# Modulation weights multiplied beside layer 0's MLP by GpSimd instead of beside its first projection by TensorE

## The chip, the cores and the metric

One core of a Trainium2 chip runs the program. The metric is the time of one execution on the device, in microseconds (us).

## The reference, cut to what matters

A diffusion backbone of two layers works on 1024 latent and 256 context tokens of 1024 features, in float32. Layer 0 is attention (GQA beside MLA) followed by a squared-ReLU MLP, layer 1 is a long convolution beside a state-space scan, again followed by an MLP. Every sub-layer is modulated by vectors that depend on the conditioning alone:

```
cond_x = silu(c);  cond_c = silu(c_ctx)
for i in range(2):
    mx = split(cond_x @ ada_w[i] + ada_b[i], 6)      # shift, scale, gate of mixer, then of MLP
    mc = split(cond_c @ ada_w[i] + ada_b[i], 6)      # the same for the context stream
    hx = rms_norm(x, g[0]) * (1 + mx[1]) + mx[0]
    x = x + mx[2] * rms_norm(mixer(hx), g[1])
    x = x + mx[5] * rms_norm(mlp(rms_norm(x, g[2]) * (1 + mx[4]) + mx[3]), g[3])
    # the context stream the same way in layer 0; in layer 1 only its first shift and scale are needed
```

`ada_w` is 1024 x 6144 for each layer. The kernel handles it in 12 pieces of 1024 x 512 (2 MB) for each layer, 24 in all. Pieces 0 and 1 are the mixer's shift, 2 and 3 its scale, 4 and 5 its gate, 6 to 11 the same three for the MLP.

## The kernel before, in words

Tokens are cut into three chunks of 512, 512 and 256 columns; features lie in eight tiles of 128 partitions. An exact product is made of three fp32r matmuls for each pair of tiles: weight high part by data high part, high by low, low by high. So each weight tile is rounded by ScalarE (ACT) and its rest is made by VectorE (DVE), `w_low = w_raw - w_high`. Engines run their own instruction lists in order and meet in semaphores; all DMAs are issued by SyncE (SP), in the order of its list.

**The modulation** (class `Modulation`, L102 to L181). For one piece: `load` (L132, a 2 MB DMA into a ring of three), `multiply` (L143: eight matmuls on TensorE (PE), conditioning as weights, four column groups side by side; each shows as two records), `copy` (L153: ACT, PSUM to rows), `turn` (L162: four matmuls that turn the rows into columns), `bias` (L173 on DVE, with L179 or L181 where a norm's gain is folded in).

**The opening** (`opening`, L189). The norm of x: squares (ACT L266), their sum over features (PE L241), the root (ACT L273, L275), scaling (DVE L322), shift and high part (ACT L284), low part (DVE L327), chunk after chunk. The first four pieces of `ada_w` come before anything can be scaled. Pieces 4 to 9 of the list `ADA_FIRST` are made between: ACT copies one after each third shift (`AFTER`). ACT's list squares all eight tiles of chunk 1, then shifts four of chunk 0, takes the root, shifts the other four, and so on.

**The first projection** (`project_attention`, L400): 5 weight tiles by 3 chunks are 15 steps, each 24 matmuls (L396), the sum of squares by head (L476) and the swap for the rotary part (L483), two steps behind. In each of the first 14 steps PE also runs `ada.turn(step - 1)` and `ada.multiply(step)` for the 14 pieces of `ADA_LATER`.

**The joined stage** (`out_and_mlp`, L1316), once for each layer, is one list of steps. In layer 0: steps 0 to 23 are the output projection (eight weight tiles for each chunk, L1568), 24 to 87 the MLP of chunk 0, 88 to 151 that of chunk 1, 152 to 215 that of chunk 2, which has 256 columns; 216 to 227 the next layer's projection. In an MLP four steps "up" (L1581) and four "down" (L1598) alternate. Weights (512 KB a step, SP L1470) go through two raw buffers: the load for step i + 3 waits until DVE has split the tile of step i + 1 (L1741), ACT rounds it (L1648). Norm jobs run beside: POOL (GpSimd) adds the squares of the output (L1853) and of x (L1878) and adds the stream to gated output (L1870); DVE gates (L1759), scales (L1783) and makes low parts (L1752). On PE, `spread_sums` (L1546, L1556) sums what POOL has added, inside a step:

```
pe.wait_ge(added_out, (KT - 1) * (q + 1) - closing[q])
...
pe.wait_ge(added_x, (KT - 1) * (q + 1))
```

Job 0, the norm of chunk 0 ahead of its MLP, has its gates and squares at steps 8 to 13, beside the output projection. ACT squares an output tile into one of two buffers and so waits until POOL has added the tile two before it.

## Time and profile before

| | |
|---|---|
| three runs | 3461.07, 3456.45, 3459.39 us; median 3459.39 |
| profiled execution, first to last instruction | 3457.7 us |
| its time around that span | not recorded apart; the median is 1.7 us above the span |
| PE, DVE, ACT, POOL busy | 96%, 53%, 37%, 20% of the span |
| mean granted TensorE clock | 0.984 of full speed |

A busy share is an average over stages; which engine sets the pace of a stage is read from the waits and the timeline of that stage. In the profile a time stands in us from the start of the span, and "idle before" is the time for which the engine did nothing ahead of an instruction, with the name of what it waited for.

### The profile page before, as it was taken

The numbers are of one execution on the slowest core, as the hardware profiler recorded it, in microseconds if no ns is written. First come the engines' busy times: TensorE is split into PE (matmuls) and PEld (weight loads), VectorE is DVE, ScalarE is ACT, GpSimd is POOL, SyncE is SP. The second block draws the span as 40 slices with busy tenths as digits, with TensorE's granted clock in tenths as the row PEclk, the third lists the DMA queues.
The fourth block names the chain that finished last, engine by engine and source line by source line (L and its number), as shares of the span: only waits on it lengthen the run. The fifth ranks groups of instructions, "written<-read, shape, count | busy, mean of one in ns | idle before, by whom it ended". The sixth has DMA issues, their size and how long they took to land. (4 is left out here: it accounts for less than half of the span.)

```text
span 3457.7 us, 39533 instructions
## 1 busy us (share of the span) xinstructions
PE 3317.7 (96%) x15472; PEld 2443.2 (71%) x15472; DVE 1818.6 (53%) x2304; ACT 1291.3 (37%) x2118; POOL 691.5 (20%) x383
## 2 busy tenths in 40 slices
PE   6999999999999999999999999898999999999998
PEld 3666444555788888888889878652456788888886
DVE  3233544433555544554586444588576654445444
ACT  4333344445553333333454223452113532233332
POOL 0000478667331101300120100110011320002001
PEclk8999999999999999999999999999999999999999
DMA  8753533321253333433465311102513333333333
GB/s 329 290 214 103 179 65 77 77 61 48 98 171 127 112 97 97 146 98 96 131 195 175 113 62 39 51 1 101 203 49 109 132 126 97 98 98 117 121 98 104
DMA packets 134552, 406.62 MB, mean 118 GB/s; under 512 B 24153, under 2 KB 38265, under 8 KB 130016
## 3 DMA queue, kind: packets, MB, share of 16 engines
q1 hardware_dynamic: 134368, 404.11, 36.1%
q8 instruction: 123, 2.02, 0.2%
q14 instruction: 61, 0.50, 0.0%
HBM read 345.05 MB, written 58.92 MB: 117 GB/s over the span
## 5 line engine op out<-in xcount | busy, mean ns | idle before, releaser
L1598 PE MATMUL psum<-hid_high,w_high_and_low 128*128 128x512 f32 (+1 forms) x1536 | 416.3, 356 | 11.7 <-DVE hid_low L1831 9.4
L1581 PE MATMUL psum<-h_high,w_high_and_low 128*128 128x512 f32 (+1 forms) x1536 | 415.6, 356 | 0.7 <-DVE w_high_and_low L1741 0.7
L1648 ACT ACTIVATE w_high_and_low<-w_raw 128x1024 fp32r<-128x1024 f32 x226 | 238.6, 1056 | 342.3 <-PE psum L1598 238.8
L1853 POOL TENSOR_TENSOR squares_then_rstd_of_out<-squares_then_rstd_of_out,square_out 128x512 f32<-128x512 f32 (+1 forms) x69 | 103.2, 1495 | 1277.1 <-ACT square_out L1663 1277.1
L1741 DVE TENSOR_TENSOR w_high_and_low<-w_raw,w_high_and_low 128x1024 fp32r<-128x1024 f32 x226 | 285.7, 1265 | 90.9 <-ACT w_high_and_low L1648 90.2
L1313 POOL TENSOR_TENSOR probs_added<-probs_added,probs_turned 128x1024 f32<-128x1024 f32 x128 | 308.1, 2407 | 66.6 <-ACT probs_turned L1238 54.0
L1598 PEld LDWEIGHTS psum<-hid_high,w_high_and_low 128*128 128x128 f32 x1536 | 274.2, 190 | 54.5 <-DVE hid_low L1831 7.8
L1581 PEld LDWEIGHTS psum<-h_high,w_high_and_low 128*128 128x128 f32 x1536 | 273.1, 189 | 42.5 <-DVE w_high_and_low L1741 1.3
L1280 DVE TENSOR_REDUCE row_max<-psum 128x1 f32<-128x1280 f32 x120 | 179.0, 1492 | 228.5 <-PE psum L1176 137.2
L1828 DVE TENSOR_TENSOR hid_high<-hid_relu_and_square 128x512 fp32r<-128x512 f32 (+1 forms) x160 | 111.5, 697 | 351.3 <-ACT hid_relu_and_square L1731 351.2
L1598 PE MATMUL psum<-hid_low,w_high_and_low 128*128 128x512 f32 (+1 forms) x768 | 272.2, 354 | 0.0
L1581 PE MATMUL psum<-h_low,w_high_and_low 128*128 128x512 f32 (+1 forms) x768 | 271.7, 354 | 0.0
L1238 ACT ACTIVATE probs_turned<-psum 128x512 f32<-128x512 f32 (+1 forms) x352 | 189.3, 577 | 198.1 <-PE psum L1143 183.9
L1731 ACT ACTIVATE hid_relu_and_square<-psum 128x512 f32<-128x512 f32 (+1 forms) x160 | 88.5, 553 | 409.9 <-PE psum L1581 409.8
L1581 PE MATMUL psum<-h_high,first_w_high_and_low 128*128 128x512 f32 x688 | 218.1, 391 | 0.0
L1598 PE MATMUL psum<-hid_high,first_w_high_and_low 128*128 128x512 f32 x672 | 211.8, 390 | 0.0
L1153 PE MATMUL psum<-probs_turned,v_pair 128*64 128x512 f32 (+1 forms) x704 | 164.8, 589 | 0.8 <-ACT attended L1245 0.8
L1581 PEld LDWEIGHTS psum<-h_low,w_high_and_low 128*128 128x128 f32 x768 | 145.2, 189 | 21.2 <-issue 1.2
L1598 PEld LDWEIGHTS psum<-hid_low,w_high_and_low 128*128 128x128 f32 x768 | 145.9, 190 | 20.2 <-issue 0.2
L1648 ACT ACTIVATE first_w_high_and_low<-w_raw 128x1024 fp32r<-128x1024 f32 x94 | 99.0, 1053 | 161.2 <-PE psum L1598 157.7
L1841 DVE TENSOR_TENSOR mixed<-mixed,psum 128x512 f32<-128x512 f32 (+1 forms) x168 | 97.7, 596 | 109.8 <-PE psum L1598 109.5
L1581 PEld LDWEIGHTS psum<-h_high,first_w_high_and_low 128*128 128x128 f32 x688 | 129.2, 188 | 29.9 <-issue 0.5
(472 smaller groups left out, 6713.0 us busy)
## 6 DMA issues: line engine op xcount, KB each, us to landing
w_raw<-in_ff_w_dram SPq DMA_DIRECT2D x320, 512.0 KB, 3.6
ada_ring<-in_ada_w_dram SPq DMA_DIRECT2D x24, 2048.0 KB, 9.8
w_raw<-in_w_out_dram SPq DMA_DIRECT2D x38, 512.0 KB, 3.5
scratch_spectra<-spectrum_out SPq DMA_DIRECT2D x32, 256.0 KB, 2.0
filter_ring<-scratch_spectra SPq DMA_DIRECT2D x16, 512.0 KB, 3.9
stream_in<-scratch_x SPq DMA_DIRECT2D x27, 256.0 KB, 4.4
w_raw<-in_w_hy_dram SPq DMA_DIRECT2D x12, 512.0 KB, 3.9
scratch_hyena<-mixed SPq DMA_DIRECT2D x12, 512.0 KB, 2.6
```

Source lines behind the costliest of these rows:

```text
L1153: mm = pe.matmul(g.ps[64 * h:64 * h + 64, V_BANK, 0:nq], v[:, pair % 2, kt, h, :], pt[:, i % RING, h, 0:nq], start=(kt == lo), stop=(kt == ...
L1238: act.activation(pt[:, i % RING, h, 0:nq], g.ps[:, T_BANKS[(2 * i + h) % 3], 0:nq], ACT.Exp).then_inc(exped, 1)
L1280: dve.tensor_reduce(neg_max[:, u % 2, 4 * h + t:4 * h + t + 1], flat[:, 0:TOK], AX.X, ALU.max, negate=True).then_inc(maxed, 1)
L1313: pool.tensor_tensor(total, old, pt[:, i % RING, :, 0:nq], ALU.add).then_inc(added, 1)
L1581: mm = pe.matmul(bank[:, 0:n], x[i % SLOTS][:, k, :], y[:, k, a:a + n], start=(k == 0 and m == 0), stop=(k == KT - 1 and m == 2))
L1598: mm = pe.matmul(bank[:, 0:n], x[i % SLOTS][:, 2 * k + half, :], y[:, k, 0:n], start=(k == 0 and m == 0), stop=(k == HT - 1 and m == 2))
L1648: act.activation(w_hi[i % SLOTS], raw[i % 2], ACT.Copy).then_inc(w_rounded, 1)
L1731: act.activation(relu[:, v % 2, 0:n], g.ps[:, u % BANKS, 0:n], ACT.Relu).then_inc(up_free, 1)
L1741: dve.tensor_tensor(w_lo[i % SLOTS], raw[i % 2], w_hi[i % SLOTS], ALU.subtract).then_inc(w_split, 1)
L1828: dve.tensor_tensor(hid_hi[:, j, 0:n], relu[:, v % 2, 0:n], relu[:, v % 2, 0:n], ALU.mult).then_inc(hid_rounded, 1)
L1841: dve.tensor_tensor(out[:, m, a:a + n], out[:, m, a:a + n], g.ps[:, u % BANKS, 0:n], ALU.add).then_inc(down_free, 1)
L1853: pool.tensor_tensor(acc_out[:, q % 2, 0:n], acc_out[:, q % 2, 0:n], sq_out[:, v % 2, 0:n], ALU.add).then_inc(added_out, 1)
```

## The change

Eight pieces are made in the opening instead of ten, two beside the first projection instead of fourteen, and the other fourteen (two of layer 0, twelve of layer 1) in the joined stage of layer 0. There each piece comes as eight granules of 128 x 512 (256 KB), 112 in all, one for a step that the list `norm_beside` leaves free: SP loads a granule once POOL is done with the one two before it; POOL multiplies it by one column of the conditioning and adds it to a sum (`tensor_scalar`, then `tensor_tensor`), for two streams in the first three batches (granules at three of four free steps), for one stream in the last two. The first granule of each piece is not added. That makes 160 `tensor_scalar` and 140 `tensor_tensor` on [128, 512]. Granules lie at steps 2, 3, 4, 6, 7, 8, 14, 15, 16, 18, 19, 20, 22, 23 and 24, then between steps 35 and 151 (77 of them), at 160 to 162 and at 179 to 195. Batches end at steps 36, 67, 97, 139 and 196: there PE sums four rows over the partitions, ACT copies, PE turns a step later, DVE adds the bias a step after that. In the opening ACT shifts tile k + 2 of chunk 0 between squares of chunk 1, and tile k of chunk 1 behind square k of chunk 2. The scratch for software-made DMA descriptors is set to 1024 bytes; every DMA here is issued by SP.

```diff
 NORM_OF = {SCALE_A: 0, GATE_A: 1, SCALE_M: 2, GATE_M: 3}
-ADA_FIRST = [(0, piece) for piece in (2, 3, 0, 1, 4, 5, 6, 7, 8, 9)]
-ADA_LATER = [(0, piece) for piece in (10, 11)] + [(1, piece) for piece in range(ADA_PIECES)]
+ADA_FIRST = [(0, piece) for piece in (2, 3, 0, 1, 4, 5, 6, 7)]
+ADA_LATER = [(0, piece) for piece in (8, 9)]
+END_OF_ADA = 212
+ADA_BESIDE = [(0, (10, 11), (0, 1)), (1, (2, 3), (0, 1)), (1, (0, 1), (0, 1)), (1, (4, 5, 6, 7), (0,)), (1, (8, 9, 10, 11), (0,))]
 
 
...
-        AFTER = {6: 4, 9: 5, 12: 6, 15: 7, 18: 8, 21: 9}
+        BIAS_AFTER = {11: 4, 17: 5, 20: 6, 24: 7}
...
-                for i in range(NEEDED, A):
+                ada.multiply(pe, 4)
+                ada.turn(pe, 4)
+                add_squares(2, range(0, 4))
+                ada.multiply(pe, 5)
+                add_squares(2, range(4, KT))
+                ada.turn(pe, 5)
+                for i in (6, 7):
                     ada.multiply(pe, i)
                     ada.turn(pe, i)
-                    if i == NEEDED:
-                        add_squares(2)
...
-                of_x(1)
-                shift(0, range(0, 4))
+                shift(0, (0, 1))
+                for k in range(KT):
+                    of_x(1, (k,))
+                    if k + 2 < KT:
+                        shift(0, (k + 2,))
                 root(1)
-                shift(0, range(4, KT))
-                of_x(2)
-                shift(1, range(0, 4))
+                ada.copy(act, 4)
+                for k in range(KT):
+                    of_x(2, (k,))
+                    if k == 5:
+                        ada.copy(act, 5)
+                    shift(1, (k,))
                 root(2)
-                shift(1, range(4, KT))
-                shift(2, range(KT))
+                ada.copy(act, 6)
+                shift(2, range(0, 5))
+                ada.copy(act, 7)
+                shift(2, range(5, KT))
...
-    units = [(i, half) for i, (c, e, j) in enumerate(steps) for half in range(1 if e is None or (c is not None and j < HT) else 2)]
+    MODS = ADA_BESIDE if ada_w is not None else []
+    norm_beside = [(KT + 1, KT + 5), (26, 35), (46, 55), (88, 96), (99, 108), (152, 160), (163, 179), (212, END_OF_ADA)]
+    quiet = [i for i in range(2, END_OF_ADA) if not any(a <= i < b for a, b in norm_beside)]
+    granules, mod_at, granule_at = [], {}, {}
+    at = 0
+    for b, (of_layer, of_pieces, streams) in enumerate(MODS):
+        for piece in of_pieces:
+            for k in range(KT):
+                if len(streams) > 1 and at % 4 == 3:
+                    at += 1
+                granule_at[quiet[at]] = len(granules)
+                granules.append((b, of_layer, piece, k))
+                at += 1
+        mod_at[quiet[at]] = b
+        at += 1
+    ops_of = [len(MODS[b][2]) * (1 if k == 0 else 2) for b, of_layer, piece, k in granules]
+    ops_by = [sum(ops_of[:m + 1]) for m in range(len(granules))]
+    batch_ops = [max(ops_by[m] for m in range(len(granules)) if granules[m][0] == b) for b in range(len(MODS))]
+    units = []
+    for i, (c, e, j) in enumerate(steps):
+        units += [(i, half) for half in range(1 if e is None or (c is not None and j < HT) else 2)]
+        if i in mod_at:
+            units.append((i, "mod"))
     unit_of = {x: u for u, x in enumerate(units)}
     through = [unit_of.get((i, 1), unit_of[i, 0]) + 1 for i in range(N)]
...
+                def load_granule(m):
+                    b, of_layer, piece, k = granules[m]
+                    if m >= 2:
+                        sp.wait_ge(mod_stepped, ops_by[m - 2])
+                    sp.dma_start(mod_raw[:, m % 2, :], ada_w[of_layer * ADA_PIECES + piece][:, k, :]).then_inc(mod_in[m % 2], 16)
+
                 for i in range(END):
                     if i + 3 > BROUGHT:
                         load_weights(i + 3)
+                    if i in granule_at:
+                        load_granule(granule_at[i])
                     for q, k in load_at.get(i, ()):
                         load_x(q, k)
...
+                def add_over_rows(i):
+                    bank = bank_for(unit_of[i, "mod"])
+                    pe.wait_ge(mod_stepped, batch_ops[mod_at[i]])
+                    for x in range(4):
+                        mm = pe.matmul(bank[32 * x:32 * x + 32, :], g.ones[:, 0:32], mod_acc[:, x, :], start=True, stop=True, tile_position=(0, 32 * x))
+                    mm.then_inc(product, 1)
+
+                def turn_rows(i):
+                    bank = g.ps[:, unit_of[i, "mod"] % BANKS, :]
+                    pe.wait_ge(mod_copied, mod_at[i] + 1)
+                    for m in range(4):
+                        mm = pe.matmul(bank[:, 4 * m:4 * m + 4], mod_row[:, m * P:(m + 1) * P], g.ident[:, 0:P:32], start=True, stop=True)
+                    mm.then_inc(mod_turned, 1)
+
                 for i in range(END):
                     if i < N:
                         if i >= MADE:
...
                     if i >= N or kind(i) in ("down", "next"):
                         spread_sums(i)
+                    if i - 1 in mod_at:
+                        turn_rows(i - 1)
+                    if i in mod_at:
+                        add_over_rows(i)
                 if NEXT:
                     pe.wait_ge(g.narrow_in, 64)
...
                         v = KT * q + k
+                        if MODS and q == C and k == 0:
+                            act.wait_ge(mod_biased, 3)
...
+                    if i in mod_at:
+                        u = unit_of[i, "mod"]
+                        act.wait_ge(product, u + 1)
+                        act.activation(mod_row[:], g.ps[:, u % BANKS, :], ACT.Copy).then_inc(mod_copied, 1)
...
+                def modulate_with(i):
+                    b = mod_at[i]
+                    of_layer, of_pieces, streams = MODS[b]
+                    n, first = len(of_pieces), of_pieces[0]
+                    turned = g.ps[:, unit_of[i, "mod"] % BANKS, 0:16]
+                    flat = g.mod[:, of_layer].rearrange("p a k s -> p (a k s)")[:, 8 * first:8 * (first + n)].rearrange("p (a m s) -> p a m s", a=n, s=2)
+                    offset = vec(g, "ada_b", 8 * (of_layer * ADA_PIECES + first), 8 * n).rearrange("p (a m s) -> p a m s", a=n, s=2)
+                    dve.wait_ge(mod_turned, b + 1)
+                    if len(streams) == 2:
+                        by_piece = turned.rearrange("p (m a s) -> p a m s", m=4, s=2)
+                    else:
+                        by_piece, flat, offset = turned.rearrange("p (m a) -> p a m", m=4), flat[:, :, :, 0], offset[:, :, :, 0]
+                    dve.tensor_tensor(flat, by_piece, offset, ALU.add).then_inc(mod_biased, 1)
+                    for part in range(first // 2, (first + n) // 2):
+                        if part in NORM_OF:
+                            dve.wait_ge(mod_biased, b + 1)
+                            gains = vec(g, "norm_g", (of_layer * 4 + NORM_OF[part]) * 16, 16).rearrange("p (k s) -> p k s", s=2)[:, :, 0:len(streams)]
+                            now = g.mod[:, of_layer, part, :, 0:len(streams)]
+                            if part in (SCALE_A, SCALE_M):
+                                dve.scalar_tensor_tensor(out=now, in0=now, scalar=1.0, in1=gains, op0=ALU.add, op1=ALU.mult).then_inc(mod_folded, 1)
+                            else:
+                                dve.tensor_tensor(now, now, gains, ALU.mult).then_inc(mod_folded, 1)
+
                 def gate_out(q, k):
                     b, m = spans[chunk[q]]
                     if k == 0:
                         dve.wait_ge(rstd_out, q + 1)
+                    if MODS and q == C and k == 0:
+                        dve.wait_ge(mod_folded, 2)
...
+                    if i - 2 in mod_at:
+                        modulate_with(i - 2)
                     for q, k in gate_at.get(i, ()):
                         gate_out(q, k)
...
+                def add_granule(m):
+                    b, of_layer, piece, k = granules[m]
+                    streams, w, n = MODS[b][2], mod_raw[:, m % 2, :], ops_by[m] - ops_of[m]
+                    pool.wait_ge(mod_in[m % 2], 16 * (m // 2 + 1))
+                    if b and granules[m - 1][0] != b:
+                        pool.wait_ge(mod_turned, b)
+                    for s in streams:
+                        total = mod_acc[:, MODS[b][1].index(piece) * len(streams) + s, :]
+                        scaled_w = total if k == 0 else w if s == streams[-1] else mod_row[:]
+                        if n:
+                            pool.wait_ge(mod_stepped, n)
+                        pool.tensor_scalar(scaled_w, w, g.cond[:, k, s:s + 1], None, ALU.mult).then_inc(mod_stepped, 1)
+                        n += 1
+                        if k:
+                            pool.wait_ge(mod_stepped, n)
+                            pool.tensor_tensor(total, total, scaled_w, ALU.add).then_inc(mod_stepped, 1)
+                            n += 1
+
                 for i in range(END):
                     for q, k in square_at.get(i, ()):
...
                         add_square_of_out(steps[i][0], steps[i][2])
+                    if i in granule_at:
+                        add_granule(granule_at[i])
 
 
```

## Rows read from the trace of the kernel before

**Rows 1.** Page, part 1: busy time and share of the span.

```profile
PE 3317.7 (96%) x15472; PEld 2443.2 (71%) x15472; DVE 1818.6 (53%) x2304; ACT 1291.3 (37%) x2118; POOL 691.5 (20%) x383
```

**Rows 2.** Stretches: window, its length, then each engine's busy time.

```profile
0.00:82.00 82.00, 54.72 (x288) 25.98 (x288) 29.86 (x63) 38.36 (x67) 0.20 (x4) 0.91 0.85 339
82.00:227.00 145.00, 135.09 (x766) 92.69 (x770) 47.15 (x90) 50.95 (x92) 0.00 (x0) 0.97 0.69 263
...
995.00:1343.00 348.00, 348.00 (x1533) 287.43 (x1532) 188.96 (x240) 124.54 (x169) 45.44 (x30) 1.00 0.36 115
...
1691.00:1902.00 211.00, 197.99 (x1567) 192.26 (x1566) 153.88 (x218) 109.77 (x165) 46.36 (x29) 0.99 0.59 184
```

**Rows 3.** Timeline of the opening, ACT and DVE: start, duration, what.

```profile
37.35 2.19 ACT L266 ACTIVATE norm_square_x<-x 128x512 f32<-128x512 f32 x4 [3.82 <-DMA x<-in_x_dram]
...
44.74 1.93 ACT L284 ACTIVATE h_high<-norm_scaled,modulation 128x512 fp32r<-128x512 f32 x3
...
48.36 0.63 ACT L275 ACTIVATE rstd_x<-rstd_x 128x512 f32<-128x512 f32 x1
...
54.17 2.07 DVE L322 SCALAR_TENSOR_TENSOR norm_scaled<-x,modulation,rstd_x 128x512 f32<-128x512 f32 x3
...
68.06 0.58 ACT L153 ACTIVATE ada_rows<-psum 128x512 f32<-128x512 f32 x1
...
77.52 0.60 ACT L153 ACTIVATE ada_rows<-psum 128x512 f32<-128x512 f32 x1 [2.67 <-PE psum L143]
...
79.95 1.27 DVE L327 SCALAR_TENSOR_TENSOR h_low<-norm_scaled,modulation,h_high 128x256 fp32r<-128x256 f32 x3
```

**Rows 4.** Timeline of PE in the first projection: one piece of the modulation.

```profile
101.82 0.95 PE L162 MATMUL psum<-group_selector,ada_rows 128*128 128x2 f32 x8
103.20 1.92 PE L143 MATMUL psum<-ada_ring,conditioning 128*32 128x512 f32 x16 [0.42 <-DVE modulation L173]
105.05 1.13 PE L476 MATMUL psum<-a_sq,ones_by_head 128*128 128x512 f32 x2
```

**Rows 5.** Groups on POOL by shape: count, then busy and mean ns.

```profile
L2338 POOL TENSOR_TENSOR x_dt<-x_tokens,dt 128x512 f32<-128x512 f32 x16 | 16.8, 1052 | 330.1 <-ACT x_tokens L2291 244.8 <-PE psum L2241 85.3
...
L2947 POOL COPY folded_turned<-folded_turned 128x1 f32<-128x1 f32 x8 | 3.4, 429 | 0.0
```

**Rows 6.** Timeline of POOL in the output projection, undisturbed and beside job 0.

```profile
921.80 1.30 POOL L1853 TENSOR_TENSOR squares_then_rstd_of_out<-squares_then_rstd_of_out,square_out 128x512 f32<-128x512 f32 x1 [4.14 <-ACT square_out L1663]
...
947.28 3.76 POOL L1878 TENSOR_TENSOR squares_then_rstd_of_x<-squares_then_rstd_of_x,square_x 128x512 f32<-128x512 f32 x2 [0.69 <-ACT square_x L1705]
951.00 1.29 POOL L1853 TENSOR_TENSOR squares_then_rstd_of_out<-squares_then_rstd_of_out,square_out 128x512 f32<-128x512 f32 x1
```

**Rows 7.** Timeline of DVE and POOL where their instructions meet.

```profile
1005.48 1.22 DVE L1741 TENSOR_TENSOR w_high_and_low<-w_raw,w_high_and_low 128x1024 fp32r<-128x1024 f32 x1
...
1005.71 2.14 POOL L1870 TENSOR_TENSOR mixed<-mixed,stream_in 128x512 f32<-128x512 f32 x1 [11.50 <-DVE mixed L1759]
...
1734.08 1.29 POOL L1870 TENSOR_TENSOR mixed<-mixed,stream_in 128x512 f32<-128x512 f32 x1 [3.35 <-DVE mixed L1759]
...
1734.28 2.18 DVE L1741 TENSOR_TENSOR w_high_and_low<-w_raw,w_high_and_low 128x1024 fp32r<-128x1024 f32 x1 [0.34 <-ACT w_high_and_low L1648]
```

**Rows 8.** Chunk 2's MLP: DVE's splits, 31 steps apart, and a rounding.

```profile
1798.26 1.23 DVE L1741 TENSOR_TENSOR w_high_and_low<-w_raw,w_high_and_low 128x1024 fp32r<-128x1024 f32 x1 [1.01 <-ACT w_high_and_low L1648]
...
1894.46 1.23 DVE L1741 TENSOR_TENSOR w_high_and_low<-w_raw,w_high_and_low 128x1024 fp32r<-128x1024 f32 x1 [1.11 <-ACT w_high_and_low L1648]
...
1797.16 1.06 ACT L1648 ACTIVATE w_high_and_low<-w_raw 128x1024 fp32r<-128x1024 f32 x1 [1.62 <-DMA w_raw<-in_ff_w_dram]
```

**Rows 9.** Page, part 6: DMA issues, count, size, median us to landing.

```profile
w_raw<-in_ff_w_dram SPq DMA_DIRECT2D x320, 512.0 KB, 3.6
...
stream_in<-scratch_x SPq DMA_DIRECT2D x27, 256.0 KB, 4.4
```

**Rows 10.** Waits of PE, 874 to 1902 us: total us, times, longest.

```profile
PE psum L1598 <- DVE hid_low L1831: 9.4, 10, 1.4
```

More of the change, by code:

```diff
@@ L235, in _, with add_squares @@
             def _(pe):
-                def add_squares(c):
+                def add_squares(c, tiles=range(KT)):
                     a, n = spans[c]
-                    for k in range(KT):
+                    for k in tiles:
                         q = c * KT + k
@@ L284, in shift @@
                         act.activation(g.high[:, k, a:a + n], t[:, q % RING, 0:n], ACT.Identity, bias=mod(SHIFT_A, k, c)).then_inc(rounded, 1)
-                        if q + 1 in AFTER:
-                            ada.copy(act, AFTER[q + 1])
                 biased_all = ada.biased
```

34 lines of the change are left out of this document (22 added, 12 removed).

## The prediction, made before the changed kernel was run

> **What bounds the kernel now.** I read the page first: PE is busy for 96% of the span [rows 1], so work taken from PE's list shortens the run unless something takes its place. Then the stretches, for the stages that the change touches [rows 2]. In the opening (0 to 82 us) PE has 54.7 us of work in 82: other things set its pace. In the first projection (82 to 227) PE is busy for 135.1 of 145 us while DVE has 47.2 and ACT 51.0: PE sets the pace. In the MLPs of chunks 0 and 1 PE has no gap (348.0 of 348, chunk 0's row). In chunk 2's MLP PE has 198.0 of 211 us and DVE 153.9. Thirty-one splits of weights there take 1894.46 - 1798.26 = 96.2 us, 3.10 us a step [rows 8]. Two raw buffers are filled (3.6 us [rows 9]), rounded (1.06 us) and split (1.23 us) [rows 8], and only then filled again: 5.9 us for two steps without the gaps between, so this ring stands nearly at the step. Last the waits of PE in the joined stage: 9.4 us in ten waits for the low part of the hidden tile [rows 10], DVE's work. Where the chain of waits could have told more it starts only in layer 1 and is no help.
>
> **The opening.** ACT squares chunk 1 at 37.35 and shifts chunk 0's first tile only at 44.74, so that DVE scales chunk 1 from 54.17, although its root was ready at 48.36 + 0.63 = 49.0 [rows 3]. With the shifts between the squares, DVE can finish chunk 0 by then: 5.2 us earlier. The root itself does not move, since PE's sums end it. At the other end, piece 9 is copied at 77.52 and the last low parts end at 81.2; piece 7, the last one that remains, was copied at 68.06 [rows 3]. Three shifts, the last low part, the turn and the bias stand behind that copy, about 3 us. That gives an end at 71, 10 us earlier. Ends of the range: 4 us (the two pieces' tail alone) and 13 (nothing but piece 7).
>
> **The first projection.** A piece costs PE its turn, a wait of 0.42 us for DVE's bias, and its multiplication: from 101.82 to 105.05, 3.23 us [rows 4]. Twelve pieces go: 38.8 us. What would be late next is ACT or DVE, at half PE's time before [rows 2]; a step of 512 columns shrinks from some 10.5 to 7.3 us, still above their 3 to 4 us a step. I take 38, with 32 and 40 as ends. Twelve 2 MB loads leave as well; they only make room.
>
> **What PE gets in the joined stage.** A batch is eight records of the kind of which sixteen take 1.92 us, so 0.96, and eight of the turn's kind, 0.95 [rows 4]: 1.9 us, five times, 9.6 us. In chunks 0 and 1 nothing hides it, PE has no gap there. ACT's copy and DVE's three small adds lie beside products; a bank is held for two steps of a ring of six. Ends: 7 (part of it in gaps) and 14 (waits around each).
>
> **What POOL and SP get.** A two-input POOL instruction on [128, 512] takes 1.30 us undisturbed [rows 6]. The trace has no multiplication by a column on POOL. Its bounds are 0.43 us (a copy of one column) and 1.30; nearest is the product of 512 elements with a short, repeated operand, 1.05 us [rows 5], and I take that. So a granule for two streams is 2 x 1.05 + 2 x 1.30 = 4.7 us, for one stream 2.35. All 300 instructions are 160 x 1.05 + 140 x 1.30 = 350 us. The Trainium skill (GPSIMD Engine Reference, section 4.1) calls a one-input operation on GpSimd roughly line-rate; an estimate of 0.6 us from that would make the load 278 us, and no row here shows such an instruction. The same section says to keep elementwise additions off GpSimd, at about half VectorE's speed; that speaks against the change only if POOL's time is ever waited for, which is the question below.
>
> Collisions come on top. A POOL addition that starts 0.23 us into a split takes 2.14 us, and a split that starts 0.20 us into a POOL addition takes 2.18 instead of 1.22 [rows 7]. One waits until the other is through: 0.85 us for POOL, 0.96 for DVE. So both engines get later.
>
> Four places can hand this on to PE:
>
> - **Job 0.** POOL's work in steps 2 to 8 is seven additions (9.1 us), one short granule (2.1) and five full ones (23.5): 34.7 us before collisions, in seven steps of 1.30 + 4.14 = 5.44 us [rows 6], 38.1. With collisions it comes into step 9 some 5 us late. From there to step 13 it is nearly full: 0.69 us of idle ahead of the pair at 947.28, done at 951.04 [rows 6], while PE's sum over x inside step 13 is due at about 952.4 (step 7 ended at 921, and six steps less a quarter follow). I take 3 us (0 to 8).
> - **Output projection of chunk 2**, steps 16 to 23 at about 3.1 us: POOL has six granules (28 us) and eight additions (10) in 25 us, 13 us too much. ACT cannot square more than two tiles ahead of POOL and rounds weights in the same list, two steps ahead of PE; some 9 us of slack. I take 4 us (0 to 12).
> - **MLPs of chunks 0 and 1.** Three two-stream granules need 14 us in four steps of 21.8; this fits. The low part of the last hidden tile can come later by a collision. 2 us (0 to 8), against 9.4 us of such waits now [rows 10].
> - **MLP of chunk 2**, 20 one-stream granules. POOL is busy for 2.35 of 3.1 us. In the weight ring a split waits on average perhaps 0.45 us, and a 256 KB load, 4.4 us to landing by itself [rows 9], stands in the queue with the weights: some 0.5 us a step, 10 us together with a wait for the last granule at step 196. Ends: 0, and 28 if each such step is stretched to POOL's and DVE's work end to end, 2.35 + 1.23 + 0.4 for hidden tiles = 4.0 us (18 us more than now), with 10 for the loads on top.
>
> **Sum**: -10 - 38 + 9.6 + 3 + 4 + 2 + 10 = -19.4 us. The sum starts from the profiled execution's 3457.7 us; the median of the runs is 1.7 above, so 3459.4 - 19.4 = 3440; I say 3439, a little for multiplications shorter than 1.05 us.
>
> **Rivals.**
>
> *A: stalls of 9 to 31 us, my forecast*, 3428 to 3451. For it: POOL's load beside the short steps. Chance 0.50.
>
> *B: the load is hidden*, stalls of 0 to 9 us: 3459.4 - 48 + 9.6 + 4 = 3425. For it: the step list keeps granules away from the norm jobs, POOL is at 45.4 us of 348 in chunk 0's MLP [rows 2], and every price of POOL above is on the upper side. Against it: job 0's margin of 1.4 us and the ring of chunk 2. Chance 0.27.
>
> *C: POOL and DVE block each other throughout*, stalls of 31 to 45 us, 3451 to 3466, most likely 3456. The Trainium skill (SBUF, State Buffer, section "Who interferes with whom") states the rule more widely than the rows: any GpSimd instruction that reads SBUF against any VectorE instruction with two SBUF inputs, and the second one blocks fully. The rows show it for two-input POOL instructions only; if the 160 multiplications block too, then DVE's splits and hidden tiles meet POOL for most of chunk 2's MLP, which then takes its upper end, 28 us, and the others some 10 more. Chance 0.13.
>
> *D: slower, through SP's list.* SP waits in a granule's load until POOL has done the one two before, and the weights of the next steps are queued behind it in the same list. Once POOL's pace per granule is longer than the steps it has, PE runs at POOL's pace. With three granules in four steps of 5.44 us there are 7.25 us for one; 4.7 are planned, so it decides from a mean collision of 0.64 us for each POOL instruction. At 0.85, the one seen [rows 7], a granule is 8.1 us: 48 x 0.85 = 41 us, and in chunk 2 steps of 4.0 instead of 3.1 us give 20 x 0.9 = 18 us, so 3459.4 - 38.4 + 59 = 3480. Against it: POOL's instruction meets a split only while one runs, 1.2 of 5.44 us. Chance 0.10.
>
> *The change does less than it says*: if the moved shifts gain nothing because PE's sums hold the root, the opening gives 5 us, not 10, inside the ranges above.
>
> **The numbers.** Predicted 3439 us. The range of 3417 to 3457 takes A, nearly all of B (down to a saving of 53 with 10 added) and the larger half of C. A measurement of this kernel tells 0.2%, 7 us, from no change. Faster by more: A, B and a little of C, 0.79; within: 0.11; slower: 0.10.
>
> **What would show it.** In the changed profile the first projection should take about 107 us, with PE's L396 steps of 512 columns 7.3 us apart; the opening should end at 71. In the joined stage look for PE's waits: for POOL's sum of squares at step 13, for L1741 and hidden tiles in chunk 2, for POOL at step 196; and for SP's waits on POOL. Chunk 2's steps should be 3.6 us apart where granules lie. I am wrong if the multiplication on POOL takes 0.6 us and PE's waits stay as they were (B), or if SP's weight loads run behind POOL in the 5.44 us steps (D).

## The result, and the profile after

The changed kernel takes 3469.06 us (median of 5 runs, 3468.16 to 3474.51), the kernel before 3456.7 us (5 runs, 3455.77 to 3461.07). The ratio is 1.0036 with a 95% interval of 1.0024 to 1.0049. The forecast was 3439 us in a range of 3417 to 3457: the result lies above the range, and the kernel became slower where a gain was forecast. The profiled execution of after spans 3467.2 us against 3457.7.

The page of after, part 1, beside [rows 1]: POOL's busy time went from 691.5 to 1204.3 us, PE has 256 records less but is busy for only 16 us less.

```profile
PE 3301.5 (95%) x15216; PEld 2434.0 (70%) x15216; DVE 1875.4 (54%) x2295; ACT 1286.4 (37%) x2109; POOL 1204.3 (35%) x683
```

The stretches of after, with the columns of [rows 2]: window, length, busy time (and records) of PE, PEld, DVE, ACT and POOL, then PE's granted clock, DMA share and GB/s.

```profile
0.00:71.00 71.00, 48.08 (x240) 21.64 (x240) 29.40 (x60) 36.68 (x66) 0.19 (x4) 0.92 0.83 332
71.00:178.00 107.00, 98.77 (x465) 74.10 (x466) 42.76 (x72) 43.61 (x79) 0.00 (x0) 0.95 0.34 121
...
823.00:944.00 121.00, 110.18 (x521) 91.45 (x522) 71.36 (x75) 61.76 (x104) 89.94 (x55) 0.95 0.42 136
944.00:1285.00 341.00, 326.32 (x1445) 266.92 (x1444) 198.90 (x223) 118.30 (x166) 245.88 (x156) 0.97 0.44 136
1285.00:1682.00 397.00, 397.00 (x1762) 326.34 (x1761) 212.71 (x243) 134.13 (x174) 229.93 (x133) 1.00 0.44 139
1682.00:1912.00 230.00, 206.36 (x1585) 199.71 (x1584) 171.04 (x221) 111.88 (x166) 117.66 (x68) 0.95 0.61 192
```

The first two are as forecast: 71 instead of 82 us, 107 instead of 145. In the joined stage PE now has gaps in the stretch that ends the output projection and runs through chunk 0's MLP (326.32 of 341 us busy, where [rows 2] had no gap), and chunk 2's MLP takes 230 us instead of 211, at a clock of 0.95 instead of 0.99.

To place the loss, one event that both traces have was followed: DVE's splits of the weight tiles in the joined stage (L1741 before, L1817 after), counted in their order. What stands below is worked out from the starts of those instructions in the two timelines (after minus before; the stretch's loss is the difference of two entries).

| up to the split of | before | after | difference | lost since | forecast |
|---|---|---|---|---|---|
| the first split | 886.08 | 834.91 | -51.2 | | |
| the 15th, at the end of step 15 | 967.38 | 926.85 | -40.5 | 10.7 | 3 |
| the 25th, behind chunk 2's output projection | 1000.43 | 974.49 | -25.9 | 14.6 | 4 |
| the 88th, end of chunk 0's MLP | 1343.17 | 1330.04 | -13.1 | 12.8 | 1 + 2 batches |
| the 152nd, end of chunk 1's MLP | 1693.15 | 1684.37 | -8.8 | 4.3 | 1 + 2 batches |
| the 216th, end of chunk 2's MLP | 1900.69 | 1910.95 | +10.3 | 19.1 | 10 + 1 batch |
| the last | 2011.86 | 2021.66 | +9.8 | -0.5 | |

The joined stage loses 61 us, more than the 51.2 that were won ahead of it. The forecast for it was 28.6: 9.6 for the batches and 19 for stalls.

How the 61 us divide on PE: from 874 to 1902 us the kernel before had PE busy for 1013.3 of 1028 us, from 823 to 1912 us the kernel after for 1039.9 of 1089. So PE idles 49.1 instead of 14.7 us, 34.5 more, and is busy for 26.5 us more, of which the five batches should take 9.6. The other 17 us are the same products at a lower granted clock. Here are PE's waits of after from 820 to 1912 us (who waits, for whom; total us, times, longest).

```profile
PE psum L1650 <- DVE hid_low L1934: 15.4, 7, 3.5
PE psum L1633 <- DVE w_high_and_low L1817: 9.4, 5, 6.4
PE psum L1669 <- POOL ada_added L1973: 8.3, 2, 4.8
PE psum L1598 <- POOL squares_then_rstd_of_out L1956: 5.8, 1, 5.8
PE psum L1620 <- DVE w_high_and_low L1817: 4.2, 5, 1.4
...
PE psum L1608 <- POOL squares_then_rstd_of_x L1999: 2.9, 2, 2.0
```

Against [rows 10] the wait for the hidden tile grew from 9.4 to 15.4 us with a longest of 3.5 instead of 1.4. New are the waits for POOL itself (17 us in three lines) and one of 6.4 us for a split.

The granted clock shows what such waits cost beside their own length. These are 5-us windows of after: an ordinary one, the one behind the 6.4 us wait, and the one that begins with the end of a wait for a batch's sum.

```profile
900.00:905.00 5.00, 5.00 (x24) 4.14 (x23) 3.41 (x3) 3.19 (x5) 4.93 (x3) 1.00 0.29 70
...
960.00:965.00 5.00, 5.00 (x13) 3.87 (x13) 1.13 (x1) 0.06 (x1) 4.74 (x4) 0.52 0.31 105
...
1215.00:1220.00 5.00, 4.76 (x15) 2.56 (x16) 1.20 (x1) 1.54 (x2) 0.09 (x1) 0.50 0.02 3
```

At 1.00 (2.4 GHz) PE gets 24 records done in 5 us, at 0.52 (nearly all at 1.2 GHz) 13. Summed as (1 - clock) x 5 us over all windows of the joined stage, 27.3 us are lost so in after and 5.1 us before.

What POOL's instructions cost, by groups (count | busy, mean ns | idle before and its releasers):

```profile
L1969 POOL TENSOR_SCALAR ada_raw<-ada_raw,conditioning 128x512 f32<-128x512 f32 x98 | 195.4, 1994 | 101.4 <-DMA ada_raw<-in_ada_w_dram 95.2 <-POOL ada_added L1973 1.9 <-POOL ada_added L1969 0.2
L1973 POOL TENSOR_TENSOR ada_added<-ada_added,ada_raw 128x512 f32<-128x512 f32 x98 | 140.1, 1430 | 8.2
L1969 POOL TENSOR_SCALAR ada_scaled_then_rows<-ada_raw,conditioning 128x512 f32<-128x512 f32 x42 | 84.0, 2000 | 40.4 <-DMA ada_raw<-in_ada_w_dram 37.1 <-POOL ada_added L1973 3.1 <-POOL ada_added L1969 0.2
L1973 POOL TENSOR_TENSOR ada_added<-ada_added,ada_scaled_then_rows 128x512 f32<-128x512 f32 x42 | 58.0, 1381 | 3.5
L1969 POOL TENSOR_SCALAR ada_added<-ada_raw,conditioning 128x512 f32<-128x512 f32 x20 | 38.1, 1907 | 58.5 <-PE psum L1676 43.1 <-DMA ada_raw<-in_ada_w_dram 14.3 <-POOL ada_added L1973 0.5
```

The 300 instructions take 515 us where 350 were planned. The timeline shows both prices undisturbed, and the first lateness: the last sum of squares of chunk 0's output ends at 879.2, and PE, in step 8, has waited 5.77 us for it.

```profile
877.97 1.26 POOL L1956 TENSOR_TENSOR squares_then_rstd_of_out<-squares_then_rstd_of_out,square_out 128x512 f32<-128x512 f32 x1
879.21 1.56 POOL L1969 TENSOR_SCALAR ada_scaled_then_rows<-ada_raw,conditioning 128x512 f32<-128x512 f32 x1
880.85 1.27 POOL L1973 TENSOR_TENSOR ada_added<-ada_added,ada_scaled_then_rows 128x512 f32<-128x512 f32 x1
...
879.28 2.07 PE L1598 MATMUL psum<-squares_then_rstd_of_out,all_ones 128*128 128x512 f32 x2 [5.77 <-POOL squares_then_rstd_of_out L1956]
```

A multiplication by a column takes 1.56 us, more than the two-input addition (1.27), and 1.98 on average. The longest wait for a split has its chain in the timeline too. A granule's load stands between two weight loads in SP's list (SPq is SP's queue):

```profile
951.18 0.33 SPq L1550 DMA_DIRECT2D ada_raw<-in_ada_w_dram  x1
951.55 0.91 SPq L1512 DMA_DIRECT2D w_raw<-in_ff_w_dram  x2
951.88 0.38 ACT L1733 ACTIVATE square_out<-psum 128x256 f32<-128x256 f32 x1 [2.86 <-POOL squares_then_rstd_of_out L1956]
956.69 1.06 ACT L1718 ACTIVATE w_high_and_low<-w_raw 128x1024 fp32r<-128x1024 f32 x1 [4.42 <-DMA w_raw<-in_ff_w_dram]
957.70 0.72 POOL L1956 TENSOR_TENSOR squares_then_rstd_of_out<-squares_then_rstd_of_out,square_out 128x256 f32<-128x256 f32 x1
957.78 1.73 DVE L1817 TENSOR_TENSOR w_high_and_low<-w_raw,w_high_and_low 128x1024 fp32r<-128x1024 f32 x1 [7.77 <-ACT w_high_and_low L1718]
958.40 2.54 POOL L1969 TENSOR_SCALAR ada_scaled_then_rows<-ada_raw,conditioning 128x512 f32<-128x512 f32 x1
959.56 0.80 PE L1633 MATMUL psum<-h_high,w_high_and_low 128*128 128x512 f32 x1 [6.36 <-DVE w_high_and_low L1817]
```

The weight load went out at 951.55 right behind a granule's load, which had itself been held for 7.8 us by POOL (the longest such wait). ACT's rounding waited 4.42 us for the weights, and PE got the tile at 959.56. ACT, which rounds weights in the same list, had also been held for 2.86 us by POOL's squares. And there are collisions: the split began while POOL added squares and took 1.73 instead of 1.22 us, POOL's multiplication began inside the split and took 2.54 instead of 1.56.

SP waited about 94 us for POOL in this stage, which is what rival D describes (its largest part, 83.1 us, is shown with the last experiment). The trace alone left four suspects: the loads, POOL's lateness through SP's list, its lateness through ACT's and PE's lists, and collisions between POOL and DVE.

### The profile page after: what moved, and what is told of

It is laid out like the page before. It is cut to its first block and busy times, and to the rows that moved or that the text cites. A ratio compares the mean times of both kernels' runs of the same rounds, so it can differ in the third digit from the quotient of the medians.

```text
span 3467.2 us, 39493 instructions
## 1 busy us (share of the span) xinstructions
PE 3301.5 (95%) x15216; PEld 2434.0 (70%) x15216; DVE 1875.4 (54%) x2295; ACT 1286.4 (37%) x2109; POOL 1204.3 (35%) x683
## 3 DMA queue, kind: packets, MB, share of 16 engines
q8 instruction: 121, 1.98, 0.2%
## 5 line engine op out<-in xcount | busy, mean ns | idle before, releaser
L1650 PE MATMUL psum<-hid_high,w_high_and_low 128*128 128x512 f32 (+1 forms) x1536 | 426.1, 362 | 18.3 <-DVE hid_low L1934 15.4
L1817 DVE TENSOR_TENSOR w_high_and_low<-w_raw,w_high_and_low 128x1024 fp32r<-128x1024 f32 x226 | 309.2, 1368 | 106.9 <-ACT w_high_and_low L1718 105.3
L1931 DVE TENSOR_TENSOR hid_high<-hid_relu_and_square 128x512 fp32r<-128x512 f32 (+1 forms) x160 | 128.8, 805 | 334.5 <-ACT hid_relu_and_square L1803 334.1
L1969 POOL TENSOR_SCALAR ada_raw<-ada_raw,conditioning 128x512 f32<-128x512 f32 x98 | 195.4, 1994 | 101.4 <-DMA ada_raw<-in_ada_w_dram 95.2
```

The lines of the kernel that those rows point to most:

```text
L1650: mm = pe.matmul(bank[:, 0:n], x[i % SLOTS][:, 2 * k + half, :], y[:, k, 0:n], start=(k == 0 and m == 0), stop=(k == HT - 1 and m == 2))
L1817: dve.tensor_tensor(w_lo[i % SLOTS], raw[i % 2], w_hi[i % SLOTS], ALU.subtract).then_inc(w_split, 1)
L1931: dve.tensor_tensor(hid_hi[:, j, 0:n], relu[:, v % 2, 0:n], relu[:, v % 2, 0:n], ALU.mult).then_inc(hid_rounded, 1)
L1969: pool.tensor_scalar(scaled_w, w, g.cond[:, k, s:s + 1], None, ALU.mult).then_inc(mod_stepped, 1)
```

## The experiments

Each ratio is to the kernel before on the same chip, whose median was between 3454.6 and 3456.4 us there. "Saved" and "cost" between two experiments are differences of medians.

### What is won, and what is lost to which part

No granule at all; the columns of the fourteen pieces stay zero:

```diff
-out_and_mlp(..., [d["w_xbc"][t] for t in range(2)], d["ada_w"])
+out_and_mlp(..., [d["w_xbc"][t] for t in range(2)])
```

> Leaves the fourteen pieces of the joined stage out altogether (their columns are zeros), and keeps the opening and the first projection of the changed kernel. It measures the gross saving. All theories: the joined stage of layer 0 takes what it took before (1137 us from its first product to the last split), so 51 us less than the kernel before, 3405 us. If it takes more, some of the loss comes from elsewhere than the granules.

Measured: 3404.95 us, ratio 0.9857 (0.9842 to 0.9871). The gross saving is 51 us, which is the -51.2 of the table. The joined stage's part of the change costs 3469.06 - 3404.95 = 64 us; the table has 61, as chunk 2's MLP is 3.7 us shorter in this kernel's trace than in that of before.

Granules of full size, but POOL works on 8 of 512 columns, so the rest of the modulation is missing:

```diff
-pool.tensor_scalar(scaled_w, w, g.cond[:, k, s:s + 1], None, ALU.mult)
+pool.tensor_scalar(scaled_w, w[:, 0:8], g.cond[:, k, s:s + 1], None, ALU.mult)
...
-pool.tensor_tensor(total, total, scaled_w, ALU.add)
+pool.tensor_tensor(total[:, 0:8], total[:, 0:8], scaled_w, ALU.add)
```

> As the changed kernel, with every granule loaded in full and all waits in place, but GpSimd multiplies and adds only the first 8 of 512 columns. Theory 1 (GpSimd's time, 1.56 us and more for a multiplication that I priced at 1.05, makes PE wait and its clock fall): only PE's own products remain, 10 us over e1, 3415 us. Theory 2 (the 112 loads in SyncE's list delay the weights): 30 us or more over e1, 3435 or more. Theory 3 (PE's products cost far more than 1.9 us a batch, through banks and waits): 3430 or more, with gaps around the batches.

Measured: 3416.91 us, ratio 0.9891 (0.9876 to 0.9905). Loads, lists, PE's batches and POOL's 300 instructions at this small width (157 us busy together) cost 12 us; the width of POOL's instructions costs 52. In its trace a batch shifts the stage by 2.2 us, so the five take 11.

The reverse, POOL at full width and 8 columns loaded:

```diff
-sp.dma_start(mod_raw[:, m % 2, :], ada_w[...][:, k, :])
+sp.dma_start(mod_raw[:, m % 2, 0:8], ada_w[...][:, k, 0:8])
```

> As the changed kernel, but each granule's load brings only 8 of 512 columns (32 bytes a partition); GpSimd's instructions have their full size, on zeros elsewhere. Theory 1: nearly the time of the changed kernel, 3460 to 3469 us. Theory 2: most of the loss is gone, 3425 to 3440 us.

Measured: 3465.44 us, ratio 1.0027 (1.0017 to 1.0038). Nearly all of the loss stays without the loads' bytes. Transfers are not the main cause: by the medians 3.6 us are theirs.

### Where in the stage it is lost

Eight pieces beside, from step 35 on, one stream each; the six others go back to the first projection:

```diff
-ADA_LATER = [(0, piece) for piece in (8, 9)]
+ADA_LATER = [(0, piece) for piece in (8, 9, 10, 11)] + [(1, piece) for piece in range(4)]
-ADA_BESIDE = [(0, (10, 11), (0, 1)), (1, (2, 3), (0, 1)), (1, (0, 1), (0, 1)), (1, (4, 5, 6, 7), (0,)), ...]
+ADA_BESIDE = [(1, (4, 5, 6, 7), (0,)), (1, (8, 9, 10, 11), (0,))]
-norm_beside = [(KT + 1, KT + 5), (26, 35), ...]
+norm_beside = [(0, 35), ...]
```

> Only the eight one-stream pieces of layer 1 (4 to 11) go beside the joined stage, at steps 35 to 125, so in steps of 5.44 us alone; the other eight are made in the first projection. Computes all. Theory 1: a granule is 1.56 + 1.27 = 2.9 us in 5.44, so there is next to no stall: 11.3 us from the opening, 6 x 3.2 = 19 us from the projection, less 4 us for two batches and 2 for waits: 3432 us. Theory 2: the 64 loads still cost 64/112 of some 40 us: 3453 us.

Measured: 3427.54 us, ratio 0.992 (0.9905 to 0.9935). Six pieces back should cost 6 x 3.23 = 19 us; instead the kernel is 41.5 us faster than after. So the six pieces, and granules in the early and late steps, cost 61 us in the joined stage. By the splits that stage takes no longer here than before the change.

Twelve beside, but none before step 35:

```diff
-ADA_LATER = [(0, piece) for piece in (8, 9)]
+ADA_LATER = [(0, piece) for piece in (8, 9, 10, 11)]
-ADA_BESIDE = [(0, (10, 11), (0, 1)), (1, (2, 3), (0, 1)), ...]
+ADA_BESIDE = [(1, (2, 3), (0, 1)), ...]
-norm_beside = [(KT + 1, KT + 5), (26, 35), ...]
+norm_beside = [(0, 35), ...]
```

> Pieces 10 and 11 of layer 0 go back to the first projection and the other twelve start at step 35, so that no granule lies in the output projection. Computes all. In the changed trace 25 of the 61 us lost in the joined stage lie ahead of step 24. Theory 1a (they come from granules in those steps, by way of job 0 and the short steps of chunk 2's output): 3469 - 25 - 2 for a batch + 6 for two pieces in the projection = 3448 us. Theory 1b (a backlog of GpSimd costs PE the same wherever it is met, since the rest is only moved): 3460 or more.

Measured: 3449.36 us, ratio 0.9977 (0.9968 to 0.9987). It saves 19.7 us while two pieces back cost PE 6.5 less their batch of 2.2: some 24 us were lost by the granules at steps 2 to 24, against 10.7 + 14.6 = 25.3 us in the table. Chunk 2's MLP, which still has its granules, loses 20.5 us here by its splits, as in after (19.1).

### What of it is POOL's price, and what is collision

The multiplication written as a two-input product with the column repeated:

```diff
-pool.tensor_scalar(scaled_w, w, g.cond[:, k, s:s + 1], None, ALU.mult)
+pool.tensor_tensor(scaled_w, w, g.cond[:, k, s:s + 1].to_broadcast([P, BANK]), ALU.mult)
```

> The changed kernel with GpSimd's multiplication by a column written as a two-input product with the column repeated, the form that took 1.05 us in the scan. Computes all. If it takes 1.05 to 1.30 us instead of 1.56, GpSimd gets 40 to 80 us less work, and by theory 1 some half of the loss goes: 3440 to 3452 us. If the form costs as much as the one it replaces: 3465 to 3470.

Measured: 3454.06 us, ratio 0.9997 (0.9987 to 1.0006): no longer slower than before, and 2 us above what was expected. From its trace, two such multiplications that nothing disturbs, and the largest group:

```profile
871.67 1.04 POOL L1969 TENSOR_TENSOR ada_scaled_then_rows<-ada_raw,conditioning 128x512 f32<-128x512 f32 x1
874.16 1.04 POOL L1969 TENSOR_TENSOR ada_raw<-ada_raw,conditioning 128x512 f32<-128x512 f32 x1
...
L1969 POOL TENSOR_TENSOR ada_raw<-ada_raw,conditioning 128x512 f32<-128x512 f32 x98 | 132.8, 1355 | 136.8 <-DMA ada_raw<-in_ada_w_dram 132.6
```

The same arithmetic takes 1.04 us undisturbed instead of 1.56, and 1.355 instead of 1.994 on average. The multiplications save 102 us of POOL's time, all 300 instructions together only 86 (429 instead of 515), since the additions met more collisions and got longer. That is worth 15 us of the kernel's time, more than the whole loss of 12 us against before. But 1.04 us is also the price that the prediction had assumed (1.05): with it the kernel takes 3454, not 3439 us.

Both together, eight beside and the product by a repeated column:

> Both: eight one-stream pieces beside, and the product with the column repeated. Computes all. GpSimd has room in every step already, so by theory 1 the product's price hardly counts: 3425 to 3428 us, as without it.

Measured: 3425.25 us, ratio 0.9911 (0.9896 to 0.9926). It is 31 us faster than before and 44 faster than after; where POOL has room its price hardly counts (3427.54 us with the dearer product). Its waits in the same stage:

```profile
PE psum L1650 <- DVE hid_low L1930: 7.6, 12, 1.2
...
SPq L1550 <- POOL ada_added L1969: 3.2, 4, 0.8
```

PE's longest wait for the hidden tile is 1.2 us, as before the change, SP hardly waits, and the clock loses 3.4 us instead of 27.3.

The opening alone, with every other piece in the first projection:

> The opening alone as changed; the other sixteen pieces are made in the first projection, none beside the joined stage. Computes all. The opening's 11.3 us less two pieces at 3.2 us: 3456.4 - 11.3 + 6.4 = 3451.5 us. If the opening's gain came from the smaller number of pieces and is lost with them, 3456 or more.

Measured: 3452.66 us, ratio 0.999 (0.9981 to 1.0), 1.2 us above the expectation, which takes 11.3 us as the opening's gain and 6.4 as the cost, in the projection, of the two pieces that it gives up.

POOL's instructions replaced by ones that only write and take about as long, so that no granule enters the modulation:

```diff
-pool.tensor_scalar(scaled_w, w, g.cond[:, k, s:s + 1], None, ALU.mult)
+pool.memset(mod_acc[:], 0.0)
...
-pool.tensor_tensor(total, total, scaled_w, ALU.add)
+pool.memset(mod_acc[:, 0:3], 0.0)
```

> The changed kernel with each of GpSimd's 300 instructions for the granules replaced by one that only writes: 2048 columns of zeros instead of the multiplication, 1536 instead of the addition. The modulation of layer 1 is left out by this. Theory 1c (the loss is GpSimd's lateness in its own list, whoever makes it late): if the writes take about as long as the products did, 1.6 and 1.3 us, nearly the same loss, 3455 to 3469 us. Theory 4 (the loss is the collisions at SBUF, GpSimd and VectorE each waiting for the other's instruction to end, which writes alone need not do): splits of 1.22 us again beside granules and 3420 to 3435 us. If the writes turn out far shorter than the products the run can't tell them apart by its time.

Measured: 3448.24 us, ratio 0.9973 (0.9961 to 0.9985), between the two expectations. POOL's groups in its trace and then DVE's rows for the hidden tile in layer 0, of this kernel and, in a second fence, of after:

```profile
L1969 POOL MEMSET ada_added<- 128x2048 f32 x160 | 289.9, 1812 | 206.6 <-DMA ada_raw<-in_ada_w_dram 157.2 <-PE psum L1676 42.9
L1973 POOL MEMSET ada_added<- 128x1536 f32 x140 | 193.6, 1383 | 8.1
...
L1931 DVE TENSOR_TENSOR hid_high<-hid_relu_and_square 128x512 fp32r<-128x512 f32 x64 | 44.4, 694 | 170.8 <-ACT hid_relu_and_square L1803 170.8
```

```profile
L1931 DVE TENSOR_TENSOR hid_high<-hid_relu_and_square 128x512 fp32r<-128x512 f32 x64 | 54.4, 850 | 150.1 <-ACT hid_relu_and_square L1803 150.0
```

POOL is occupied for 484 us (515 in after), yet DVE is not slowed at all: 694 ns, as with no granules. Both kinds of loss are real. Against the 3416.91 us of the kernel with 8 columns, a POOL that is busy for 484 us and blocks nobody costs 31 us, and after costs 21 more. The 21 are likely too small for the collisions: without them the multiplications and additions would be 427 us (160 x 1.56 + 140 x 1.27), less than the 484 that the writes take, so a POOL of that length alone should cost under 31. The Trainium skill (SBUF - State Buffer, section "Who interferes with whom") says that a GpSimd operation which reads SBUF and a VectorE operation with two SBUF inputs exclude each other. The trace agrees, for the one-input multiplication too: the overlap at 957.78 and 958.40 above, and 850 against 694 ns here.

The splits place what is left of the loss, one trace each (us lost in the stretch, the five batches of 2.2 us included):

| stretch, up to split | after | column repeated | only writes |
|---|---|---|---|
| 15th (job 0) | 10.7 | 6.4 | 5.1 |
| 25th (chunk 2's output projection) | 14.6 | 11.4 | 12.3 |
| 88th (chunk 0's MLP) | 12.8 | 6.8 | 6.9 |
| 152nd (chunk 1's MLP) | 4.3 | 4.3 | 4.3 |
| 216th (chunk 2's MLP) | 19.1 | 15.3 | 9.3 |

Without collisions chunk 2's output projection loses nearly as much as in after, so there POOL's lateness is the greater part; chunk 2's MLP loses half, so there the collisions weigh most.

### Is the middle load free, and is the order of the shifts worth something

Ten beside, to step 151, and the product by a repeated column:

> Ten pieces beside, all of them between steps 35 and 148: one batch for two streams and two for one, with the repeated column. Computes all. Against eight (3425 us): two pieces less in the projection, -6.4, a batch more, +2.2, and a two-stream granule of four instructions at 1.3 to 1.5 us, 5.6 us at three of four steps of 5.44. Theory 1: it fits, 3421 us. If such granules cost PE something even in long steps, 3425 to 3430.

Measured: 3424.88 us, ratio 0.9911 (0.9896 to 0.9926), equal to eight and with it the fastest of the complete kernels; of the expectations it is the second, that such granules cost something even in long steps. By the splits the joined stage begins 3.9 us earlier than with eight, less than the 6.5 that two pieces take in the projection, and takes 3.8 us longer, of which a batch is 2.2.

The kernel with eight, with the old order of the opening. That is ACT's squares and shifts (below) and also ACT's copies, PE's pieces and sums and DVE's biases, which all go back together:

```diff
-shift(0, (0, 1))
-for k in range(KT):
-    of_x(1, (k,))
-    if k + 2 < KT:
-        shift(0, (k + 2,))
-root(1)
+of_x(1)
+shift(0, range(0, 4))
+root(1)
+shift(0, range(4, KT))
```

> The eight-beside kernel with the repeated column, but with the opening's old order (all squares of a chunk ahead of the shifts of the one before) and still eight pieces. Computes all. It splits the opening's 11.3 us: if the order brings the start of chunk 1 forward by 5 us and the two pieces the rest, 3425 + 5 = 3430 us; if PE's sums hold the end anyway, 3426.

Measured: 3434.87 us, ratio 0.9936 (0.992 to 0.9953). The new order as a whole is worth 9.6 us by the medians, more than either expectation (5 and 1). At the first product of the projection it is 6.7 us, 81.34 against 74.62 (this kernel first, then the one with eight, in a fence of its own); where the other 2.9 come from is not shown:

```profile
81.34 0.79 PE L399 MATMUL psum<-h_high,w_high 128*128 128x512 f32 x1 [11.81 <-DVE w_low L388]
```

```profile
74.62 0.80 PE L409 MATMUL psum<-h_high,w_high 128*128 128x512 f32 x1 [5.73 <-DVE w_low L398]
```

### Is it SP's list

Rival D says that weight loads queue behind a granule's load that waits for POOL. A third granule buffer takes that wait away. To make room for it, `TURNS` is 2 instead of 3 in both kernels, the control without the buffer first:

```diff
-EIGHTHS, PIECES, HT, BANKS, TURNS, RING, SLOTS = 8, 8, 4, 6, 3, 3, 3
+EIGHTHS, PIECES, HT, BANKS, TURNS, RING, SLOTS = 8, 8, 4, 6, 2, 3, 3
```

> Control for the next run: the changed kernel with two instead of three buffers for scaled x (TURNS = 2), which frees the room for a third granule buffer. Computes all. All theories: as the changed kernel or a little slower, 3468 to 3475 us.

```diff
-if m >= 2:
-    sp.wait_ge(mod_stepped, ops_by[m - 2])
-sp.dma_start(mod_raw[:, m % 2, :], ...)
+if m >= 3:
+    sp.wait_ge(mod_stepped, ops_by[m - 3])
+sp.dma_start(mod_raw[:, m % 3, :], ...)
```

> The same with three granule buffers, so that SyncE waits for the granule three before instead of two before. GpSimd's work and its collisions are unchanged. Computes all. Theory 1d (GpSimd's lateness reaches PE by SyncE's list, where the weights stand behind the granule's wait): against the control 10 us or more are gained, 3460 us or less, and SyncE's waits for GpSimd (93 us in the changed kernel) shrink by half. Theory 1e (it reaches PE by ACT's and PE's direct waits on GpSimd, and by the collisions): within 4 us of the control.

Measured: 3465.95 us (1.0034, 1.0022 to 1.0045) for the control and 3469.78 us (1.0038, 1.0023 to 1.0053) with the third buffer. First SP's largest wait for POOL in after, then waits of the control, then the same with three buffers:

```profile
SPq L1550 <- POOL ada_added L1973: 83.1, 27, 7.8
```

```profile
SPq L1550 <- POOL ada_added L1973: 66.0, 26, 7.5
...
ACT squares_then_rstd_of_x L1770 <- POOL mixed L1991: 14.7, 3, 7.6
...
ACT square_out L1733 <- POOL squares_then_rstd_of_out L1956: 12.3, 4, 6.0
...
PE psum L1650 <- DVE hid_low L1934: 15.2, 9, 3.9
PE psum L1633 <- DVE w_high_and_low L1817: 8.1, 4, 6.4
```

```profile
SPq L1550 <- POOL ada_added L1973: 13.4, 7, 3.8
...
ACT square_out L1733 <- POOL squares_then_rstd_of_out L1956: 19.7, 4, 5.9
ACT squares_then_rstd_of_x L1770 <- POOL mixed L1991: 19.7, 3, 12.5
...
PE psum L1650 <- DVE hid_low L1934: 20.3, 10, 8.0
...
PE psum L1633 <- DVE w_high_and_low L1817: 3.6, 2, 2.4
```

Fifty us of SP's waits go, and nothing is gained. The path through SP's list is real at one place: PE's wait of 6.4 us for a split, in front of which a weight load had stood behind a waiting granule, shrinks to 2.4 at most. But some 30 us later ACT waits 12.5 instead of 7.6 us for POOL, which works on granules from 976.8 to 990.5 us before it comes to the stream's additions (L1991) in its list; behind that wait stands the hidden tile in ACT's list, and PE waits 8.0 instead of 2.9 us for its low part. What the third buffer gives back at one place, POOL's list takes at the next. SP's waits were for the most part a symptom.

## Why the prediction was wrong, step by step

**The opening** (-10 forecast): right, -11.3 us (PE's first product of the projection at 85.67 before, 74.39 after). The order of the shifts was forecast at 5.2 us; the old order of the whole opening costs 6.7 at the first product, and the shifts were not tested by themselves.

**The first projection** (-38): right, -51.2 + 11.3 = -39.9 us, and 51 us together by the kernel without granules. No other engine took PE's place.

**The batches** (+9.6): 11 us, 2.2 each.

**The first step that failed is POOL's price**: "The trace has no multiplication by a column on POOL. Its bounds are 0.43 us ... and 1.30; nearest is the product of 512 elements with a short, repeated operand, 1.05 us". The multiplication takes 1.56 us undisturbed, outside the bounds, since I took the two-input instruction for the dearest form. The rule of the Trainium skill that stood behind it (GPSIMD Engine Reference, section 4.1: one-input operations roughly line-rate) pointed further off; by its estimate of 0.6 us I would have been more wrong. Undisturbed the load is 160 x 1.56 + 140 x 1.27 = 427 us, not 350; collisions make it 515. The price makes the difference between slower and level, and 15 of the 30 us between forecast and result: with the form that does take 1.04 us the kernel equals the one before.

**The other 15 us failed at the assumed price too**: in that kernel stalls and clock take 33 us of the joined stage beside the batches in the one trace (44.3 up to the 216th split, less 11), and 38 by the medians, where the sum had 19. Of the 14 us too much in the trace 11 are in two of the four places, whose slack was overrated:

**Job 0** (+3): 10.7 us, and 6.4 with the cheaper product. I had looked for the deadline at step 13, where PE sums x. The first one is at step 8, where it sums the output's squares: five granules stand in POOL's list ahead of the last of those, and "comes into step 9 some 5 us late" should have been read there. PE's wait was 5.77 us.

**Chunk 2's output projection** (+4): 14.6 us, and 11.4 with the cheaper product. The excess of 13 us over the steps was worked out, then 9 us of slack were set against it. The rounding of weights stands in ACT's list with the squares, and the weights' loads in SP's list with the granules'; the split that PE waited for came 6.4 us late.

**MLPs of chunks 0 and 1** (+2): 17.1 less four batches of 2.2 is 8.3 us, nearly all in chunk 0. **Chunk 2's MLP** (+10): 19.1 less one batch is 16.9, inside its bounds of 0 and 28.

**A term that the sum did not have** is PE's granted clock. Behind a wait of some us PE ran at 1.2 GHz for a stretch. In this stage 27.3 us are lost that way instead of 5.1, 22.2 more, beside the 34.5 us more of idle time (part of the 22.2 falls into idle time; 17 us show in PE's busy time). I priced each wait at its length. That the clock fell because of the waits is read from the windows and goes with every experiment (3.4 us lost where the waits are short, 18.8 in the kernel that only writes), but it was not tested by itself.

**The rivals.** C (mutual blocking, most likely 3456) names one of the two causes rightly, worth some 21 us or more. D (slower) had the side right, but not its sum. Its threshold, a mean collision of 0.64 us for each instruction, was not reached (1.98 - 1.56 = 0.42 for the multiplications, 1.42 - 1.27 = 0.15 for the additions), and a granule for two streams took 6.8 us of the 7.25 that it had; SP's list did hold PE up at one place, yet with SP's waits mostly taken away the time stayed. The other cause is POOL's lateness, handed on through its own list to ACT and PE, up to 31 us. B (hidden) holds for part of the change: eight or ten pieces in the long steps cost little beside what they win.

What stays open: how the losses divide between the waits for POOL's sums and those for rounding and hidden tiles behind ACT's waits for POOL, since one sets off the other; how much is collisions beyond the 21 us; and why ten pieces are no better than eight.

## What to carry to other kernels

Before work is moved to an idle engine, list the deadlines of what that engine already does, in the order of its list, and put the new work only where the next deadline is far: here the long middle steps took eight pieces, and the kernel with them is 31 us faster than before; six more, which put 35 granules into the steps up to 24 and into chunk 2's MLP, turned the same idea into a loss. Count a wait of several us on PE at its length plus the half clock behind it. A price that the trace doesn't show needs an upper bound beyond the dearest similar instruction, above all where it is multiplied by 160; a second form of the same operation may be cheaper.

## What the runs showed of the hardware that was not expected

- On GpSimd a [128, 512] float32 multiplication by a per-partition column took 1.56 us, the two-input addition of that size 1.27, and the multiplication with the column repeated as second input 1.04 (1.29 to 1.36 on average in its three groups, collisions included).
- Instructions on GpSimd that only write SBUF, 1.4 to 1.8 us long and 300 of them, left VectorE's two-input instructions on [128, 512] at 694 ns; ones that read brought the mean to 850 ns.
- After waits of 3.5 and 6.4 us PE's granted clock was 0.50 and 0.52 (1.2 GHz) over a window of 5 us.
